# A block with 256 gathered expert rows: U and V fetched by one gather of 16 KB instead of two of 8 KB, and each row weighed as soon as it is summed

## The reference, cut to what matters

```python
s_top, i_top = lax.top_k(half_scores, PEER_TOPK)
cand = s_top[:, :, 0, :, None] + s_top[:, :, 1, None, :]
best, pos = lax.top_k(cand, PEER_TOPK)
gates = jax.nn.softmax(best, axis=-1)
act = jnp.einsum('td,thkd->thk', xb, u_tab[ib])
w = gb * jax.nn.gelu(act, approximate=False)
out = jnp.einsum('thk,thkd->td', w, v_tab[ib])
```

## Time and profile before

| | |
|---|---|
| median of 3 runs | 2284.51 us (2283.59 to 2287.14) |
| the profiled execution | 2281.45 us, span 2279.8 us |
| PE | 1931.5 us busy, 85% |
| DVE | 1365.9 us, 60% |
| POOL | 782.3 us, 34% |
| ACT | 390.9 us, 17% |
| HBM | 858.35 MB read, 378 GB/s over the span |
| chain that ended last | PE 43%, DMA 32%, DVE 10%, issue 7%, POOL 5% |

### The profile page before, as it was taken

The page is one execution under the profiler, slowest core; times in us unless marked ns, Lnnn a source line. Parts: engine busy times, 40 slices in busy tenths (PEclk is TensorE's granted clock), DMA queues, the critical chain, the costliest instruction groups (busy, mean ns, idle before and its releaser), DMA issues.

```text
span 2279.8 us, 27813 instructions
## 1 busy us (share of the span) xinstructions
PE 1931.5 (85%) x10646; PEld 1309.7 (57%) x10646; DVE 1365.9 (60%) x2008; ACT 390.9 (17%) x1004; POOL 782.3 (34%) x554
## 2 busy tenths in 40 slices
PE   4899899998999999989888888888884888997455
PEld 4788688887888888878645445555650222221001
DVE  7821378776444531246798889777875444443664
ACT  0112212211000001021232212544530000000011
POOL 1000000000000000004364556766878644554783
PEclk9999999999999999999999999898975999998556
DMA  9963366575676656318799999999999999999997
GB/s 390 428 271 143 125 264 246 216 293 198 234 284 242 235 207 258 145 68 354 299 380 414 407 405 414 405 398 396 393 405 356 410 417 414 400 413 352 362 354 278
DMA packets 104604, 722.42 MB, mean 317 GB/s; under 512 B 29740, under 2 KB 29740, under 8 KB 32060
## 3 DMA queue, kind: packets, MB, share of 16 engines
q0 software_dynamic: 78800, 466.66, 52.0%
q1 hardware_dynamic: 25696, 254.35, 28.0%
HBM read 858.35 MB, written 4.19 MB: 378 GB/s over the span
## 4 chain that ended last, share of the span: by engine, by line
PE 43%; DMA 32%; DVE 10%; issue 7%; POOL 5%; ACT 2%; POOLq 0%; SPq 0%; DVEq 0%
PE ps L800 21%; DMA arena<-expert_u,expert 13%; DMA arena<-expert_v,expert_q 13%; PE ps L808 10%; DMA mod_rows<-expert_u,expert 4%; POOL arena L491 4%; PE ps L997 3%; PE ps L824 3%; PE ps L1025 3%; DVE work L1446 2%; PE ps L1079 2%; DMA arena<-ada_early 2%; DVE mod_rows L1201 1%; POOL mod_rows L491 1%; DVE work L1257 1%
## 5 line engine op out<-in xcount | busy, mean ns | idle before, releaser
L1446 DVE CUSTOM_DVE_ANT_0 work<-arena,buf_b 128x2048 f32<-128x2048 f32 x166 | 381.0, 2295 | 268.4 <-DMA arena<-expert_u,expert 267.5
L997 PE MATMUL ps<-arena,mod_rows 128*32 128x512 f32 x1640 | 265.5, 727 | 208.1 <-DMA arena<-expert_v,expert_q 172.8
L800 PE MATMUL ps<-buf_a,arena 128*128 128x256 f32 x1920 | 422.9, 382 | 6.1 <-DVE arena L1275 5.3
L800 PEld LDWEIGHTS ps<-buf_a,arena 128*128 128x128 f32 x1920 | 366.7, 192 | 56.8 <-issue 6.7
L491 POOL DMA_INDIRECT arena<-expert_v,expert_q x205 | 333.7, 1628 | 166.1 <-PE ps L997 105.0
L491 POOL DMA_INDIRECT arena<-expert_u,expert x205 | 269.4, 1314 | 235.8 <-DVE work L1446 121.7
L478 POOL DMA_DIRECT2D arena<-ada_late x32 | 16.9, 529 | 771.2 <-DVE mod_rows L1201 642.1
L1025 PE MATMUL ps<-arena 128*128 128x256 f32 x1024 | 273.0, 418 | 4.7 <-DMA arena<-dense_u 4.7
L1025 PEld LDWEIGHTS ps<-arena 128*128 128x128 f32 x1024 | 202.7, 206 | 126.8 <-issue 93.0
L997 PEld LDWEIGHTS ps<-arena,mod_rows 128*32 128x32 f32 x1640 | 37.3, 117 | 342.1 <-DMA arena<-expert_v,expert_q 273.2
L655 ACT ACTIVATE work<-work 32x4 f32<-32x4 f32 (+3 forms) x320 | 66.3, 207 | 552.3 <-DVE work L1446 545.0
(11 more groups left out here) (250 smaller groups left out, 2090.6 us busy)
## 6 DMA issues: line engine op xcount, KB each, us to landing
arena<-weights SPq DMA_DIRECT2D x62, 2048.0 KB, 7.9
arena<-ada_late POOLq DMA_DIRECT2D x32, 2048.0 KB, 9.8
arena<-ada_early SPq DMA_DIRECT2D x16, 2048.0 KB, 17.8
arena<-dense_u SPq DMA_DIRECT2D x32, 1024.0 KB, 9.1
arena<-expert_v SPq DMA_DIRECT2D x32, 1024.0 KB, 8.9
arena<-w_early SPq DMA_DIRECT2D x8, 1536.0 KB, 9.7
arena<-expert_u,expert POOLq DMA_INDIRECT x205, 17.8
arena<-expert_v,expert_q POOLq DMA_INDIRECT x205, 17.5
```

Source lines behind the costliest of these rows:

```text
L800: last = mm(ps[:, bank, c * TOKENS:(c + 1) * TOKENS], ring[slot][:, first + k, c * P:(c + 1) * P], rhs[:, k, :], start=(k == 0), stop=(k = ...
L997: last = mm(ps[j * GROUP:(j + 1) * GROUP, n // HEADS * QUADS + g, :], spread_w[n % 2][:, e, :], v_slot[row % V_RING][:, j * QCOLS:(j + 1) ...
L1446: v.tensor_tensor_reduce(out=products[n > 2], in0=u_slot[s], in1=h2[:, n // HEADS], scale=1.0, scalar=0.0, op0=ALU.mult, op1=ALU.add, accu ...
```

## The change

U and V tables are joined on the host into one table `expert_rows` of 16 KB rows. One gather by the quads' index brings both parts of a row, so 256 gathers take the place of 512. Both parts lie in one of 5 places of 16 KB a partition, and a place is free when PE has added its V part. The product with U is now made in quads too, for which `h2` is stored to DRAM and loaded back four times over for each group of 32 tokens (`h2_quads`, 4 tiles of 1 MB for a block). ACT does GELU, gate and spreading for each row in three small activations (`weigh_row` in ACT's program); DVE's `weigh` and the 16 activations of `gelu` are gone.

```diff
...
-            def gather_row(table, indices, n, e, slots, row_used, row_loaded):
...
+            for n, e in row_order:
+                row = n * TOPK + e
...
+                if row == PLACES - 1:
+                    wait_alone(pool, s_h2s, 16 * BLOCKS)
+                wait_alone(pool, uv_used[row % PLACES], 1 + row // PLACES)
+                column = n % HEADS * TOPK + e
+                pool.indirect_dma_start(place[row % PLACES], None, expert_rows,
+                                        bass.IndirectOffsetOnAxis(ap=expert_q[:, n // HEADS, column:column + 1], axis=0),
+                                        bounds_check=GATHERED - 1, oob_is_err=False)\
+                    .then_inc(uv_loaded[row % PLACES], 16)
...
+            def weigh_row(n, e):
+
+                row = n * TOPK + e
+                column = n % HEADS * TOPK + e
+                own = slice(e, e + 1)
+                act_e.wait_ge(s_act, row + 1)
+                run(gel[:, own], act[:, own], ACT.Gelu).then_inc(s_gelu, 1)
+                act_e.wait_ge(s_gelu, row + 1)
+                run(wgt[:, own], gel[:, own], ACT.Copy, scale=gates_q[:, n // HEADS, column:column + 1]).then_inc(s_wgt, 1)
+                act_e.wait_ge(s_wgt, row + 1)
+                run(spread_w[row % PLACES], same_token, ACT.Copy, scale=wgt[:, own]).then_inc(s_spr, 1)
...
-                pe.wait_ge(v_loaded[row % V_RING], 16 * (row // V_RING + 1))
...
+                pe.wait_ge(s_spr, row + 1)
                 for j in range(QUADS):
...
+                    last = mm(ps[j * GROUP:(j + 1) * GROUP, g, :], spread_w[row % PLACES],
+                              v_part[row % PLACES][:, j * QCOLS:(j + 1) * QCOLS],
                               start=n % HEADS == 0 and e % QUADS == 0, stop=False, skip_group_check=True)
...
+                last.then_inc(uv_used[row % PLACES], 1)
...
+                if row:
+                    dve.wait_ge(s_act, row)
+                dve.wait_ge(uv_loaded[s], 16 * (row // PLACES + 1))
+                v.tensor_tensor_reduce(out=products[n > 2], in0=u_part[s], in1=h2_quads[g], scale=1.0, scalar=0.0,
+                                       op0=ALU.mult, op1=ALU.add, accum_out=act[:, e:e + 1]).then_inc(s_act, 1)
...
```

```diff
...
+            def load_half_tile(i):
+
+                a, half = i // 2, i % 2
+                sp.wait_ge(dense_used[half], 1 + a)
+                sp.dma_start(half_tile[half], dense_u[a * P:(a + 1) * P, half * D_MODEL // 2:(half + 1) * D_MODEL // 2])\
+                    .then_inc(dense_loaded[half], 16)
...
+            def take_sums(g):
+
+                wait_for_weighed(act_e, (HEADS - 1) * TOPK + 4 * g + 3)
+                run(taken[g], ps[:, g, :], ACT.Copy).then_inc(s_taken, 1)
...
+            def restore_sums():
...
+                for g in range(QUADS):
+                    mm(ps[:, QUADS + g, :], ident, taken[g], start=True, stop=False, skip_group_check=True)
...
```

More of the change, by code:

```diff
@@ L46 @@
 N_KEYS = 128
[L47 removed]
+PLACES = 5
+ROWS = 2 * 8 * 16
 DENSE = 32
@@ L448, in _ @@
+            for a in range(2, DENSE):
+                load_v_tile(a)
             sp.wait_ge(s_mid, 16 * BLOCKS)
+            sp.wait_ge(s_dv, 1)
             for j in range(QUADS):
@@ L672, in experts_to_quads, with first_experts_to_quads @@
                 batch_to_quads(expert_q, expert, i).then_inc(s_exq, 1)
+            def first_experts_to_quads():
+                act_e.wait_ge(s_ex, 1)
+                for g in range(QUADS):
+                    for k in range(QUADS):
+                        last = run(expert_q[k * GROUP:(k + 1) * GROUP, 0, g * QUADS:(g + 1) * QUADS],
+                                   expert[g * GROUP:(g + 1) * GROUP, 0, k * QUADS:(k + 1) * QUADS], ACT.Copy)
+                        if k < QUADS - 1:
+                            me.step(last)
+                    last.then_inc(s_exq, 1)
             def gates_to_quads(i):
@@ new lines, in keep_query, with keep_scores @@
+            def keep_query(h):
+                half = 2 * h + 1
+                act_e.wait_ge(q_used[half % 3], half // 3 + 1)
+                run(pq_t[h % 2], ps[:, 6 + h % 2, :], ACT.Copy).then_inc(s_pq, 1)
+            def keep_scores(h):
+                act_e.wait_ge(s_ks, h + 1)
+                if h == 1:
+                    act_e.wait_ge(s_mid, 16 * BLOCKS)
+                for b in range(BLOCKS):
+                    last = keep(h, b, slice(0, 2))
+                last.then_inc(s_kept, 1)
@@ L1476, in add_to_rows @@
-                last.then_inc(s_mean, 1)
-            def squares_about_mean(turn, groups):
-                own = slice(groups[0], groups[-1] + 1)
+                wait_for_weighed(dve, (b * HEADS + HEADS - 1) * TOPK + (g + 1) * QUADS - 1)
+                me.link(v.tensor_tensor(xo[:, b, g], ps[:, bank_of(a), :], gate2q, ALU.mult))
+                me.link(v.scalar_tensor_tensor(out=xo[:, b, g], in0=xq[:, b, g], scalar=ALPHA, in1=xo[:, b, g], op0=ALU.mult, op1=ALU.add))
+                me.link(v.bn_stats(q_stats[:, a], xo[:, b, g]))
@@ L1481, in squares_about_mean @@
+                last = v.bn_aggr(q_mv[:, a], q_stats[:, a])
+                if any(a == groups[-1] for groups in TURNS):
+                    last.then_inc(s_mean, 1)
+                else:
+                    me.step(last)
+            def squares_about_mean(turn):
+                groups = TURNS[turn]
+                own, bank = slice(groups[0], groups[-1] + 1), bank_of(groups[0])
                 dve.wait_ge(s_mean, turn + 1)
                 dve.wait_ge(s_avg, turn + 1)
-                me.link(v.tensor_copy(q_mean[:, own], ps[:, own, 0]))
+                me.link(v.tensor_copy(q_mean[:, own], ps[:, bank:bank + len(groups), 0]))
@@ L1512, in choices @@
                     for piece, _ in enumerate(itertools.chain(choice(k), [None])):
-                        if piece == 1 and k:
+                        if piece == 1 and k > 1:
                             normed_gates(k - 1)
```

585 lines of the change are left out of this document (297 added, 288 removed).

## The result

The changed kernel takes **2363.8 us** (median of 4 runs, 2359.1 to 2370.4), the kernel before 2284.1 (4 runs): a ratio of 1.0355, 95% interval 1.034 to 1.0371. The direction was forecast, the size was not: 3.5% slower, where 0.7% was expected. The profiled execution took 2365.88 us, its span is 2364.2.

What follows compares the result with a forecast made beforehand. DMA gathers of expert rows were taken to bound the second half. Loop terms summed to 1241 us; with the first sum at 1042.5 and 15.4 us after the last landing, span 2295 and 2300 us were forecast (range 2220 to 2375).

Steps and rivals of the forecast that it cites:

- steps 0 to 22: First rows of the loop, beside query quarters: 23 steps of 5.2 us, 119.6 us.
- steps 23 to 95: 73 steps beside 22 dense U tiles: 135.8 MB at 392 GB/s, 346 us.
- Bytes: All gathers move 395.3 MB, before and after; new after the first gather are block 1's h2_quads, 4.2 MB.
- POOL: 256 gather issues instead of 512, at worst 3.3 us a row, under 3.77 us of transfer: no longer sets the pace.
- The quads: Block 1's h2_quads loads, 4.2 MB, counted by bytes within steps 96 to 153: 104.3 MB, 266 us.
- xq: Load of xq in small packets, late in the loop: 8 us for the slower rate and 5 for bytes, 13 us.
- The hold: Each of five places is held from landing through DVE, ACT, PE and POOL: 7.6 us, leaving 3.45 in flight.
- Rival C: Half U tiles land late and PE waits 1.3 us twice a tile: 28 us more, 2328 us; chance 0.10.
- rival B: Ring starves: a place is held 10 us, whole loop at 357 GB/s, 106 us more, 2406 us; chance 0.14.
- A: Ring of places holds: time in a place is hidden, 415 GB/s beside tiles, 76 us less, 2224 us; chance 0.30.
- D: Gain at the start and loss in the loop cancel, or DMA's bytes alone count: 2280 to 2290 us; chance 0.06.
- What would show it: Signs: 385 to 398 GB/s beside U and V tiles, 360 to 370 with gathers alone, last gather landing near 2280.

Runs made afterwards that it cites:

- item 5: Changed kernel with dense U loaded in quarter tiles instead of halves, 2380.7 us, or in whole tiles, 2342.9 us; landing times of gathers were compared.
- hold_plus: Changed kernel with six more linked ACT copies in each row, between Gelu and gate: 2384.9 us (one time).
- places4: Changed kernel with four places for gathered rows instead of five: 2408.6 us (one time).
- quads_whole: Changed kernel with each h2_quads tile loaded by one DMA over 128 partitions instead of four to 32 each: 2450.8 us, ratio 1.0736.

## Why the prediction was wrong

Its own sum, term by term (the last sum at 2344.6 us, the last gather landing at 2344.4):

| term | forecast | measured | difference |
|---|---|---|---|
| first sum begins | 1042.5 | 1045.4 | +2.9 |
| steps 0 to 22 | 119.6 | 126.2 | +6.6 |
| steps 23 to 95 | 346 | 358.6 | +12.6 |
| steps 96 to 153, with the quads | 266 | 297.6 | +31.6 |
| steps 163 to 235 | 373 | 365.0 | -8.0 |
| the 29 others, with `xq`, to the last landing | 132 | 151.6 | +19.6 |
| after the last landing | 15.4 | 19.8 | +4.4 |

*Bytes* were right, 395.6 MB in the gathers' queue, and so was *POOL*: it no longer sets the pace. Its issues were stretched, to 1.6 us on average; 15 of 255 did follow the one before by 0.3 us, where the forecast had none.

*The quads* were the step that failed most. The prediction counted them as 4.2 MB at 392 GB/s (about 11 us) and did not look at the shape: 16 loads into 32 partitions. That shape cost 30 us at one time. A row of before was there to warn of it: the window of 2052 us, 352 GB/s for 410, is one in which `xq` is loaded into 32 partitions at a time. The prediction put that loss to "small packets". In the trace of before the gathered 8 KB packets took 375 ns on average in it, and 318 in 1197 to 1425 us, a sign of the same kind as 706 for 634 beside the quads. The word "narrow" is missing from the prediction.

*xq*: "8 us and its bytes 5" took the slower window of before as it stood and put the wait for the load at nothing. On record were four loads that took 26.3 us to land (median; the last landed 39 us after the first issue), and their first use 50 us after. The change moved that use to 13.5 us after the issue, between two row sums. The load stopped DVE, and with it the ring, for 26.6 us; the term had 13.

*Steps 23 to 95* were off by the half tiles. Rival C had the mechanism, round robin, and its place: PE waited for `dense_u` 26 times, 3.0 us each, where C said 1.3 us twice a tile (44 times). Total 79 us for its 57; and undoing the halves gave 21 us, near C's 28. The forecast gave C 0.10 and its own sum nothing for it. The two were not exclusive, and C's price should have stood in the sum: the rule was cited and then weighed by nothing.

*The hold* was sound in kind and wrong in its parts. The sum had 7.6 us and 3.45 places in flight throughout. Measured (5 steps less the landing, as in item 5) it was some 10 us beside U tiles, with 2.9 places in flight, and some 6 us beside V tiles, with 3.8 (landing 18.9 us, a step 5.0). The first is rival B's hold, come about by C's half tiles, though the rate fell to 379 GB/s and not to B's 357. PE's row products waited 2.1 us each time for ACT, but only 100 times in 256 rows: 0.8 us a row, where 2 to 4 were forecast. That the ring costs a share of the time and not all of it is what `hold_plus` and `places4` show, by one time each. V tiles ran at 400 GB/s in place of the 392: they come in whole tiles of 8 KB rows, 8 turns each, which fits but was not tested.

*The start.* Steps 0 to 22 took 6.6 us more than forecast. PE was busy 116 of the 126 us there, and from the first sum to that of row 22 it took 119.6 to 121.2 us in every run but `quads_whole`; what was short in the 5.2 us a step stays open. So does the 4.4 us at the end.

*Rivals.* A (2224 us) fell: the places cost something, and 377 to 379 GB/s beside weights and U tiles are not 415. Of the numbers C's (2328 us) is nearest to 2364, then B's (2406), whose 357 GB/s throughout did not come: the stretches at 317 and 259 GB/s are quads and `xq`. D fell. *What would show it* named rates of 385 to 398 beside tiles; they were 379 and 400, and an average of the two would have hidden that one is a loss and the other a gain. The direction came out in part by luck: the loss that the forecast had was the ring's rate beside tiles, while 72 us of 80 went away with three loads that its sum took by their bytes, or little more.

## What to carry to other kernels

Where two queues keep the DMA engines busy, count a load in packets per engine, not in bytes: packets of the other queue go in between, up to one for each, so a load of few bytes and many packets lands late, and later still when the other queue's packets grow (a half tile in 7.9 us beside gathers of 8 KB, in 10.4 beside 16 KB). Look at how many partitions a load writes before you cost it by its bytes, and at how long it has before its first use. When a change merges two transfers into one larger one, list the other loads that share the engines; what is won in issues may be paid there.

## What was not expected of the hardware

An 8 KB packet into 32 partitions took 510 ns, into 128 partitions 312 ns, and 16 KB packets of the other queue took 706 ns on average beside the narrow ones, 634 beside the wide. In the median a 16 KB packet took 611 ns, 8 KB 309, 4 KB 159, 2 KB 84 (U quarters) to 108 (`xq`): little is lost in rate down to 4 KB, so size matters here by turns more than by efficiency. Four DMAs with a broadcast outermost dimension of 4 held up what stood behind them in their queue, and PE waited 64 us. An issue of a gather that met no row sum on DVE took 0.99 us; beside sums issues took up to 3.1 us, and in the median the stretched ones ended 0.86 us after a sum did.
